# Recurrence gates of an RG-LRU branch: both gates of a 64-channel block in one half of TensorE's rows, two blocks on the two halves

## The reference

```
r = sigmoid(xc_block @ w_lru_a[block] + b_lru_a)
i = sigmoid(xc_block @ w_lru_x[block] + b_lru_x)
a = exp(-8 r softplus(-lambda)),   u = sqrt(1 - a^2) * (i * xc),   h_t = a_t h_(t-1) + u_t
```

## Time and profile before

| | |
|---|---|
| device time, median of 3 runs | 1840.55 us (1835.17 to 1846.29) |
| profiled execution: span, first to last instruction | 1836.7 us |
| mean granted TensorE clock | 0.980 |
| TensorE busy | 1735.7 us, 94% |
| VectorE busy | 1267.8 us, 69% |
| ScalarE busy | 1050.5 us, 57% |
| GpSimd busy | 333.6 us, 18% |
| HBM read and written | 384.06 and 51.13 MB |

### The profile page before, as it was taken

One profiled execution on the slowest core, in us unless ns is written; L12 is line 12 of the kernel. 1 busy time (PEld: TensorE's weight loads), 2 busy tenths in 40 slices (PEclk: granted clock), 3 DMA queues, 4 the chain that ended last, 5 costly groups with the idle time before them and its releaser, 6 DMA issues. The chain is left out here.

```text
span 1836.7 us, 27148 instructions
## 1 busy us (share of the span) xinstructions
PE 1735.7 (94%) x10322; PEld 1488.9 (81%) x10322; DVE 1267.8 (69%) x1656; ACT 1050.5 (57%) x1459; POOL 333.6 (18%) x336
## 2 busy tenths in 40 slices
PE   6999889999999999999999997899999999999994
PEld 3889768888888899999999986687877888788871
DVE  4524367888887634546355667789888999889966
ACT  4535345666666533435344534577787878787853
POOL 0000011111110000000001100234435443345310
PEclk9999899999999999999999998999999999999997
DMA  8554541111111853735474663889989898889867
GB/s 351 178 189 141 174 171 50 50 50 50 50 50 39 296 191 120 261 126 162 161 253 154 202 224 137 308 362 370 380 356 386 359 380 356 366 360 379 361 237 286
DMA packets 101301, 416.63 MB, mean 227 GB/s; under 512 B 16040, under 2 KB 43848, under 8 KB 87497
## 3 DMA queue, kind: packets, MB, share of 16 engines
q1 hardware_dynamic: 85488, 392.71, 57.2%
q0 software_dynamic: 10704, 17.73, 2.6%
q10 hardware_dynamic: 5016, 4.93, 0.9%
HBM read 384.06 MB, written 51.13 MB: 237 GB/s over the span
## 5 line engine op out<-in xcount | busy, mean ns | idle before, releaser
L1100 ACT ACTIVATE wup<-wraw 128x1024 fp32r<-128x1024 f32 x120 | 126.7, 1059 | 269.5 <-PE ps L1973 236.7
L1602 DVE TENSOR_TENSOR wlow<-wraw,wup 128x1024 fp32r<-128x1024 f32 x120 | 146.7, 1223 | 157.9 <-ACT wup L1100 157.5
L1753 DVE TENSOR_TENSOR wg_low<-wg,wg_up 128x2048 fp32r<-128x2048 f32 x68 | 152.9, 2288 | 28.9 <-ACT wg_up L1215 28.7
L1753 DVE TENSOR_TENSOR wu_low<-wu,wu_up 128x2048 fp32r<-128x2048 f32 x68 | 155.3, 2287 | 16.1 <-ACT wu_up L1221 15.4
L1753 DVE TENSOR_TENSOR wd_low<-wd,wd_up 128x2048 fp32r<-128x2048 f32 x66 | 148.6, 2291 | 11.9 <-ACT wd_up L1273 11.5
L1221 ACT ACTIVATE wu_up<-wu 128x2048 fp32r<-128x2048 f32 x68 | 129.9, 1913 | 26.0 <-PE ps L1973 26.0
L1215 ACT ACTIVATE wg_up<-wg 128x2048 fp32r<-128x2048 f32 x68 | 126.7, 1910 | 30.2 <-DMA wg<-w_gate 29.0
L1050 ACT ACTIVATE pp<-ps,ngm 128x256 f32<-128x256 f32 x128 | 59.5, 470 | 135.5 <-DVE skd L1487 119.8
L1973 PE MATMUL ps<-h_up,wup 128*128 128x384 f32 (+1 forms) x384 | 126.1, 328 | 3.0 <-DVE wlow L1602 3.0
L1973 PE MATMUL ps<-h_low,wup 128*128 128x384 f32 (+1 forms) x384 | 125.0, 325 | 0.0
L1973 PE MATMUL ps<-h_up,wlow 128*128 128x384 f32 (+1 forms) x384 | 125.0, 325 | 0.0
(11 more groups left out here) (391 smaller groups left out, 4829.3 us busy)
## 6 DMA issues: line engine op xcount, KB each, us to landing
wg<-w_gate SPq DMA_DIRECT2D x34, 2048.0 KB, 12.1
wu<-w_up SPq DMA_DIRECT2D x34, 2048.0 KB, 13.2
wd<-w_down SPq DMA_DIRECT2D x34, 2048.0 KB, 7.9
wraw<-w_ga SPq DMA_DIRECT2D x24, 512.0 KB, 3.8
wraw<-w_gr SPq DMA_DIRECT2D x24, 512.0 KB, 3.6
wraw<-w_at SPq DMA_DIRECT2D x24, 512.0 KB, 3.5
wraw<-w_lr SPq DMA_DIRECT2D x24, 512.0 KB, 3.5
wraw<-w_out SPq DMA_DIRECT2D x24, 512.0 KB, 3.6
```

Source lines behind the costliest of these rows:

```text
L1100: act.activation(wup[n % UP][:, :, :], wraw[n % RAW][:, :, :], ACT.Copy).then_inc(w_rounded, 1)
L1602: V.tensor_tensor(wlow[n % RAW][:, :, :], wraw[n % RAW][:, :, :], wup[n % UP][:, :, :].bitcast(F32), ALU.subtract).then_inc(w_split, 1)
L1753: V.tensor_tensor(low[:, k0:k1, :], whole[:, k0:k1, :], up[:, k0:k1, :].bitcast(F32), ALU.subtract).then_inc(done, 1)
```

## The change

The two gates of one 64-channel block now share one matmul: the weight of a block is 64 x 128, gate a in the first 64 columns and gate x in the last 64. The two blocks of a chunk lie on partitions 0 to 63 and 64 to 127, so an even output o is block 0 and an odd one block 1, each with 64 contraction rows. The output of a block has gate a in partitions 0 to 63 and gate x in 64 to 127, so each output is copied by two ScalarE instructions of 64 partitions, into the block's half of gA and of gB. The matmuls are issued in pairs: one wait before the even one for both banks, one count of 2 after the odd one. Outputs 6 and 7 stay at step 8, and 8 moves to step 9, with 9, 10 and 11. The weight tile is 128 x 128 in place of 128 x 2 x 128 and the biases are rearranged on the host.

```diff
--- before.py
+++ after.py
@@ -180,7 +180,7 @@
         a0 = zone_k + 2 * (P + TOK) + (TILES + 1) * KV
         wA, wA_low = at("wA", [P, KC, P], a0), at("wA_low", [P, KC, P], a0, F32R)
         w0 = zone_k + 2 * (P + TOK) + (TILES + 1) * KV + KC * P
-        wlg = at("wlg", [P, 2, P], w0)
+        wlg = at("wlg", [P, P], w0)
         wB, wB_low = at("wB", [P, KC, P], w0 + 2 * P), at("wB_low", [P, KC, P], w0 + 2 * P, F32R)
         tmp0 = w0 + 2 * P + KC * P
 
@@ -468,7 +468,7 @@
         def halves_at(s):
 
             return (((0, 0),), ((0, 1), (1, 0)), ((1, 1), (2, 0)), ((2, 1),), ((3, 0),), ((3, 1),), ((4, 0), (4, 1)), ((5, 0), (5, 1)),
-                    ((6, 1), (7, 1), (8, 1)), ((9, 1), (10, 1), (11, 1)))[s]
+                    ((6, 1), (7, 1)), ((8, 1), (9, 1), (10, 1), (11, 1)))[s]
 
         GC = [slice(g * GW, (g + 1) * GW) for g in range(GRP)]
 
@@ -570,7 +570,7 @@
                     for n in (14, 15):
                         ada_piece(n)
                 h_store(m - 2)
-            sp.dma_start(wlg[:, :, :], I["w_lg"][0]).then_inc(ld_wlg, 16)
+            sp.dma_start(wlg[:, :], I["w_lg"][0]).then_inc(ld_wlg, 16)
 
             def xl_weights(i):
 
@@ -581,7 +581,7 @@
             def lg_weights(i):
 
                 sp.wait_ge(proj_done, number(i - 1, 11) + 1)
-                sp.dma_start(wlg[:, :, :], I["w_lg"][i]).then_inc(ld_wlg, 16)
+                sp.dma_start(wlg[:, :], I["w_lg"][i]).then_inc(ld_wlg, 16)
 
             def yl_weights(i):
 
@@ -1021,8 +1021,12 @@
                     elif o < 6:
                         act.activation(yl[:, GC[g]], src, ACT.Copy).then_inc(proj_kept, 1)
                     else:
-                        dst, bias = ((gA, 0), (gB, 1))[o % 2]
-                        act.activation(dst[:, GC[(o - 6) // 2]], src, ACT.Tanh, bias=lcur[:, bias:bias + 1], scale=0.5).then_inc(proj_kept, 1)
+                        b, cols = o % 2, GC[(o - 6) // 2]
+                        half = slice(HD * b, HD * b + HD)
+                        for m, dst in enumerate((gA, gB)):
+                            of = slice(HD * m, HD * m + HD)
+                            ins = act.activation(dst[half, cols], ps[of, o % 3, 0:GW], ACT.Tanh, bias=lcur[of, b:b + 1], scale=0.5)
+                        ins.then_inc(proj_kept, 1)
 
             def lru_step(i, s):
 
@@ -2085,8 +2089,10 @@
             def outs(i, s):
                 for o, part in halves_at(s):
                     out = ps[:, o % 3, 0:GW]
-                    if part == 0 or o >= 6:
+                    if part == 0:
                         pe.wait_ge(proj_kept, number(i, o) - 2)
+                    if o in (6, 8, 10):
+                        pe.wait_ge(proj_kept, number(i, o + 1) - 2)
                     if (o, part) == (0, 0):
                         pe.wait_ge(p_split, PAIR[0, i + 6])
                     if (o, part) == (3, 0):
@@ -2100,7 +2106,10 @@
                         if part:
                             ins.then_inc(proj_done, 1)
                     else:
-                        mm(out, wlg[:, o % 2, :], xc[:, GC[(o - 6) // 2]], True, True).then_inc(proj_done, 1)
+                        half = slice(HD * (o % 2), HD * (o % 2) + HD)
+                        ins = mm(out, wlg[half, :], xc[half, GC[(o - 6) // 2]], True, True)
+                        if o % 2:
+                            ins.then_inc(proj_done, 2)
 
             def first_out(o):
                 pe.wait_ge(proj_kept, number(0, o) - 2)
@@ -2463,12 +2472,12 @@
     q, k, v, xl, yl, ga, gr = np.split(w_in, np.cumsum([D, KV, KV, D, D, D]), axis=1)
     q = q.reshape(D, 16, HD)[:, HEADS].reshape(D, D)
     w_at = g["w_attn_branch"][0].reshape(16, HD, D)[HEADS].reshape(D, D)
-    lg = np.zeros((KC, P, 2, P), np.float32)
+    lg = np.zeros((KC, P, P), np.float32)
     for m, name in enumerate(("w_lru_a", "w_lru_x")):
         w = g[name][0].reshape(KC, 2, HD, HD)
-        for a in range(2):
-            lg[:, a * HD:(a + 1) * HD, m, a * HD:(a + 1) * HD] = w[:, a]
-    vec = [g["b_lru_a"][0], g["b_lru_x"][0], g["lru_lambda"][0], g["b_conv"][0], *g["w_conv"][0]]
+        lg[:, :, m * HD:(m + 1) * HD] = w.reshape(KC, P, HD)
+    gates = np.stack([g["b_lru_a"][0], g["b_lru_x"][0]]).reshape(2, KC, 2, HD).transpose(2, 1, 0, 3).reshape(2, D)
+    vec = [gates[0], gates[1], g["lru_lambda"][0], g["b_conv"][0], *g["w_conv"][0]]
     sinks = g["sinks"][0]
     sink_s = np.repeat(np.broadcast_to(sinks.reshape(4, 1, 4), (4, 2, 4)).reshape(-1), NT)
     kc = g["cache_k_win"][0].reshape(NB, P, 2, P)
```

## The result

The changed kernel takes 1869.01 us (median of 4 runs, 1866.38 to 1871.96) against 1841.49 us (4 runs, 1835.17 to 1846.29): a ratio of 1.0147, 95% interval 1.0127 to 1.0168, +27.5 us. The forecast was 1853.5, its range ended at 1864. The direction was right, the size was about half.

The account below looks back on a forecast made before the run. PE, working in fixed order, was taken to bound the attention rounds. Waits of 0.2 + 6 x 1.2 + 2.3 = +9.7 us and +3.3 for the clock gave +13.0, a span of 1849.7, forecast as 1853.5 us; range 1843 to 1864.

Parts of the forecast that it names:

- PE in order sets the round, and a gain on PE counts only as far as no wait takes its place: Attention rounds: PE works in fixed order, busy 45.06 of 46.0 us; its delays lengthen the round, savings may become waits.
- Pairs overlap, 0.68 us a pair: Gate matmuls: two 64-row matmuls run side by side in 0.68 us, 0.62 up to the start of what follows.
- rival without overlap: Gate matmuls: halves run one after the other, 1.31 us a pair; +19 us, 1859.5 us, chance 0.08.
- Waits for gate 6's and gate 8's copy, about 0.8 and 2.3 us: Rounds 1 to 6: PE idles about 0.8 us before pair (8, 9) and 2.3 before pair (10, 11).
- The time goes where gate 8's copy is moved behind the tanh: End of rounds 1 to 6: gate 8's copy stands behind four half copies, tanh and head copy; +1.2 us a round.
- The copy's spacing of 0.44 us: ACT's gate copies: a half copy costs 0.44 us like a whole one, 5.3 us a round for 2.6.
- The clock, two falls, +3.3: PE's idle stretches behind the gates: the granted clock falls twice, some 1.65 us each, +3.3 us.
- the case given 0.12: Rival: the clock falls every time, in rounds 1 to 6 and the last projection; +21.3 us, 1861.9 us, chance 0.12.
- Round 7 and the merge stage, +2.3 of at most 2.8: Round 7's end: last projection starts 2.8 us later; between 0.5 and 2.8 us remains after it, 2.3 taken.
- Round 0, +0.2: Round 0, without a tanh between the copies: scores start near 270.7 instead of 270.49, +0.2 us.
- Nothing changes behind 640 us: Stages after 640 us: none changes its length; one that did would show the forecast wrong.
- The estimate of 0.85 us a pair: Gate matmuls: at 77% as from four row tiles, a pair takes 0.85 us, the sum growing by 2 to 3 us.

Follow-up runs that it names:

- e4_whole: Changed kernel with one copy of 128 partitions per gate in place of two half copies; 45.84 to 45.87 us a round, span 1836.4 us.
- e1_move: Kernel before with only gate 8 moved from step 8 to step 9; 45.88 to 45.91 us in rounds 1 to 6, 1836.95 us beside 1841.05.
- e2_halves: Kernel before with every gate copy split into two of 64 partitions, staying on their partitions; 47.3 us a round, span 1847.7 us.
- e5_warm: Changed kernel with unread matmuls that keep PE at work while it waits for copies; 1860.25 us, ratio to before 1.0087.
- e6_banks: Changed kernel with the six gate outputs in six different PSUM banks, PE's waits moved to their next users; 1852.22 us, ratio to before 1.0057.
- e3_cross: As e2_halves, but each half copy goes into the other 64 partitions; 47.4 us a round, span 1854.1 us.
- e9_cols: Kernel before with every gate copy split into two of 176 columns over all 128 partitions; 1845.35 us beside 1839.22 (one run).
- e8_tanh: e7_late with the GeLU's tanh put ahead of the copies of gates 6 and 7; 1829.99 us, ratio to before 0.9937.
- e7_late: e6_banks with gates 10 and 11 copied behind the next round's first exponential, their banks exchanged; 1846.94 us, ratio to before 1.0031.

## Why the prediction was right or wrong

- *PE in order sets the round, and a gain on PE counts only as far as no wait takes its place*: right. e4_whole is the clean case.
- *Pairs overlap, 0.68 us a pair*: they do, at 0.80 (0.62 was taken for the last one, up to the scores). The first two records of a pair start 7 ns apart, the second two 0.40 later. The rival without overlap falls.
- *Waits for gate 6's and gate 8's copy, about 0.8 and 2.3 us*: measured 0.68 (0.96 in round 6) and 2.68, in every one of rounds 1 to 6, released by ACT's copy into gB.
- *The time goes where gate 8's copy is moved behind the tanh*: half right. Alone the move costs nothing (e1_move); it needs the half copies with it, and these alone cost 1.4 us a round (e2_halves).
- *The copy's spacing of 0.44 us*: the first step that failed. I took it from whole copies and carried it to half ones because instructions of 32 and 128 partitions **last** equally long. What counts is the step from start to start, and for part of the partitions that step is the whole duration: 0.56 and 0.57. The kernel before had shown it in a row that I did not ask for: four copies of 32 partitions take 4.37 us in a row, a step of 1.10, where the tanh of 128 partitions by as many columns had one of 0.97 (timeline of ACT before):

```profile
126.08 4.37 ACT L946 ACTIVATE turned<-oT 32x1056 f32<-32x1056 f32 x4
```

Even the tanh and the head copy between the half copies stood 1.10 us apart and not 0.97. From first gate to scores 5.65 us were forecast (449.59 to 455.24) and 6.48 came: the half copies made 0.62 of the difference, the tanh 0.13, the last pair (0.80 for 0.62) 0.18, while PE started 0.05 us behind the copy and not 0.14. So +1.2 us a round became +2.04: 5 us in rounds 1 to 6.
- *The clock, two falls, +3.3*: the second step that failed, and the larger one. It fell in all six rounds and behind round 7, the case given 0.12, and in rounds 1 and 2 for 6.8 us at a time. e5_warm prices it at 1.9 us a round, 11.5 us in all (299.2 to 287.8 for rounds 1 to 6), where 3.3 was forecast. The price of a fall was about right: the four rounds with 3.4 us at the lower level lost 1.5 to 1.6 us each, for 1.65 foretold, and the two with 6.8 us lost 2.5 and 2.8. What failed is how often and how long. I had counted falls as chance; with work for PE in both idle stretches (e5_warm) there were none, without it the clock fell in each round. Either failed step alone would have stayed within the range (1861.9 with a fall every time; by an estimate from the forecast's sum, 1858.5 with 5 us more of waits); together they left it.
- *Round 7 and the merge stage, +2.3 of at most 2.8*: measured 4.4 to the last projection and 2.1 beyond it, 6.5 in all, the third term that was too small. There the clock is at its lower level for 10.2 us, and the copies are as slow as elsewhere; whole copies lose 2.9 of it (e4_whole, with 6.8 us at the lower level). 2.8 came back as shorter waits.
- *Round 0, +0.2*: measured 0.9 to 1.2, which e1_move shows to be the size of what a longer stretch at the lower clock does there; the change's own part isn't shown.
- *Nothing changes behind 640 us*: wrong by the 8.5 us above, part of which is open.
- The rule in the Trainium skill, "TensorEngine Tiling (Array Packing)", "PSUM Bottleneck", that tiling speeds the matmuls and not the emptying of PSUM, was borne out: 1.5 us a round less of PE's work, 3.6 more of ACT's (27.77 to 31.34). The estimate of 0.85 us a pair, from the 3.07x that the Trainium skill, "TensorE: Matmul & The Clock Gate", Part 3, gives for four row tiles, was near: the trace has 0.80.

## What to carry to other kernels

Before splitting an evacuation by partitions, look at the step between such instructions, not at how long one lasts: here 64 partitions by 352 columns cost 0.57 us each and 128 by 352 0.44, while a cut by columns was nearly free. Shortening the matmuls ahead of a full set of banks only lengthened the wait for the copy (e4_whole). What paid in the rounds was to give the outputs banks of their own and to put the tanh, on which VectorE's work hangs, first; banks alone lost (e6_banks). And where a change makes TensorE idle twice within a few us, work out what the lower clock costs in every repetition, not in some of them.

## What the runs showed of the hardware

- ACT's copies over 32 or 64 partitions don't overlap with the same kind behind them (steps of 0.56 to 0.57 us for a duration of 0.55, in e2_halves, e3_cross and the changed kernel; 1.10 for 1.08 over 32 partitions in the kernel before), those over 128 do (0.44 for 0.55, 0.29 for some 0.4 in e9_cols). Whether input and output are the same partitions made no difference to that. It isn't the whole rule: the tanh over 128 partitions, behind half copies and ahead of the head copy, had a step of 1.10 for 1.08 in the changed kernel, and one of 0.98 in round 7, where the rounding stands behind it. Why is open.
- Fp32 matmuls of 64 rows on the two halves of the array run side by side: of the four records of a pair two start 7 ns apart and two more 0.40 us later, 0.80 us for a pair alone and 1.39 for two pairs in a row (447.21 to 448.60 in e8_tanh).
- After 0.68 and 2.68 us of idling with 0.8 us of work between them the granted clock fell to half in all six rounds; with waits of 1.16 us (e4_whole) it fell in none of them. Behind waits of 0.77 and 1.64 us, with 7 us of work between them, it fell in three rounds of six (e7_late), so the same waits need not have the same effect each time.
